# Moving a quarter of the value-row sums from TensorE to VectorE in a PEER decoder kernel

## The chip, the cores and the metric

The kernel runs on one core of one Trainium2 chip. The metric is the device time in microseconds (us), the median of the runs shown.

## What is computed

The reference is a decoder trunk of two layers over 512 tokens of width 1024, in float32. Layer 0 mixes tokens with gated linear attention (GLA), layer 1 with sliding-window attention (SWA); after each mixer stands a PEER channel mixer. In PEER every token picks, in each of 8 heads, 16 of 16384 experts by a product-key top-k. Expert e has a row u[e] and a row v[e] of 1024 values each. A token's 128 picks give

```python
ue = u[e]
ve = v[e]
a = jax.nn.gelu(jnp.einsum('thkd,td->thk', ue, xb).astype(jnp.float32), approximate=False) * g
return jnp.einsum('thk,thkd->td', a.astype(xb.dtype), ve)
```

So each pick is a dot product with u[e], a scalar coefficient, and a scaled sum of v[e]. The rows differ from token to token, so all of them are gathered from HBM: 512 tokens x 128 picks x 2 layers x 8 KB, some 1074 MB.

## The kernel before

Tokens are in 4 blocks of 128, one token a partition. Each block and layer is a stage, 8 stages in all. A stage has two sides that run beside each other: it serves the picks of its own block, and it prepares the next block (mixer, query projection, top-k selection). The last stage has no preparation.

**Serving.** Tables u and v lie side by side, so a gather brings 8 KB a partition, 1 MB a pick. `ring` has 8 slots for them. A stage's 128 picks are 16 rounds of 8 slots, or 64 beats of 2 picks. For a pick in slot i the engines do this:
- POOL (L497) waits for `used[i]`, which says that the slot is free, and issues the gather. It takes slots in order.
- DVE (L840) waits for `got[i]` and multiplies the u row with `h_now`, with the sum in `dots`.
- ACT makes gelu (L1041), `coef`, which is gelu times gate (L1044), and `diag`, the identity scaled by `coef` (L1052). There are 4 `diag` buffers, so ACT first waits until PE has used the one of four picks ago.
- PE (L1310) multiplies `diag` with the v row in two halves of 512 columns into the PSUM tile `acc`, which gathers the sum of all 128 picks. Its last matmul increments `used[i]`.

**Preparing.** Each engine's steps carry a beat in the table `AT`; `beside` writes them into the engine's instruction stream ahead of that beat's picks, and runs rounds without a step in a hardware loop. Engines run in order, so an engine that waits in a step holds back its picks too. Steps tell each other by `said_by`. Among them are, on PE, the strips of weights (L1119, L1130: 8 or 16 matmul groups on a 1 MB strip), the output projection, whose end is the event `y`, the query projection `pq0` to `pq3` and the scores (L1298), which read `keysT`. On DVE they are the attention scores' mask and maximum (L667 to L683) and the selection from `topa0` to `keyb1` (L745 to L823), at beats 48 to 63 in layer 0 and 51 to 63 in layer 1. The one-hot (L805) and its uses lie in the `arena` at 4096. The attention groups g0 to g3 start at beats 17, 21, 25 and 29.

**Loads.** SP issues the weight strips. 8 are resident in a layer; the rest are streamed through two buffers, each when its predecessor is used or when an event such as `y` is said (`FREED`). `keysT`, 0.5 MB, has an SBUF tile of its own and is loaded once a layer.

## Time and profile before

| | |
|---|---|
| median of 3 runs | 3310.17 us (3306.16 to 3312.98) |
| span of the profiled execution | 3290.3 us |
| mean granted TensorE clock | 0.935 of full |
| data moved by DMA | 1173.69 MB, 357 GB/s on average |
| PE / DVE / ACT / POOL busy | 81% / 57% / 38% / 39% of the span |

The profile is of one execution, and its span goes from the first to the last instruction; the device time contains some 20 us around it. The stages lie in it as follows (first dot of each): stage 0 at 185 us, 1 at 584, 2 at 990, 3 at 1389, 4 at 1790, 5 at 2182, 6 at 2577, 7 at 2970. Stages 0 to 2 prepare a layer-0 block, stages 3 to 6 a layer-1 block. The names of engines are those of the profile: PE is TensorE (PEld its weight loads), DVE VectorE, ACT ScalarE, POOL GpSimd, SP SyncE. A matmul of float32 appears as several MATMUL records. A busy share says little by itself, since the stages have several stretches with different limits.

### The profile page before, as it was taken

Reading aid. Unit: us, or ns where it says so; the run is one execution under the profiler, and the core shown is the slowest. Engines: PE = TensorE matmul, PEld = TensorE weight load, DVE = VectorE, ACT = ScalarE, POOL = GpSimd, SP = SyncE. Lnnn points to the kernel's source line nnn. Section 1 sums busy time; section 2 is a strip of 40 time slices with the busy share of each in tenths; the row PEclk is TensorE's granted clock in tenths of the full one; section 3 lists DMA queues with packets and bytes.
Section 4 is the critical chain, followed back from the end, with each engine's and each line's share of the span. In section 5 each row is a group of like instructions: output and inputs, shape, how many; then the busy total and the mean of one; then the engine's idle time right before and its main releaser. Section 6 shows DMA issues by size and latency. Waiting matters only on the chain.

```text
span 3290.3 us, 33210 instructions
## 1 busy us (share of the span) xinstructions
PE 2668.6 (81%) x8416; PEld 1386.3 (42%) x8416; DVE 1876.9 (57%) x4651; ACT 1239.7 (38%) x3668; POOL 1277.0 (39%) x1186
## 2 busy tenths in 40 slices
PE   7568887888878888688896978878897788978777
PEld 6435453453534544343452434434453344533222
DVE  2564549444494455936468554775448654495444
ACT  2033423334333443335333353344433344333333
POOL 0033433334343343333344333434334343436675
PEclk9789998899989999899998999989999999989999
DMA  5388998989989899899898998989989898999999
GB/s 194 110 351 328 399 376 340 369 333 395 384 352 371 336 401 377 346 421 399 308 412 336 367 383 322 396 340 360 362 336 382 339 382 327 368 368 380 422 422 375
DMA packets 163484, 1173.69 MB, mean 357 GB/s; under 512 B 18848, under 2 KB 19104, under 8 KB 21488
## 3 DMA queue, kind: packets, MB, share of 16 engines
q0 software_dynamic: 147456, 1073.81, 81.7%
q1 hardware_dynamic: 15856, 97.88, 7.4%
q8 instruction: 72, 1.18, 0.1%
q14 instruction: 100, 0.82, 0.1%
HBM read 1167.42 MB, written 4.19 MB: 356 GB/s over the span
## 4 chain that ended last, share of the span: by engine, by line
PE 20%; DVE 14%; issue 6%; POOL 6%; DMA 3%; ACT 2%; ACTq 0%; POOLq 0%; DVEq 0%; SPq 0%
PE acc L1310 14%; POOL ring L497 6%; DVE ring L840 5%; PE ps L1130 3%; DMA ring<-in_uv,pick_now 3%; PE ps L1119 1%; DVE arena L813 1%; DVE arena L805 1%; DVE arena L817 1%; PE ps L1254 1%; DVE arena L757 1%; PE ps L1128 1%; DVE arena L749 1%; DVE arena L750 1%; ACT diag L1052 0%
## 5 line engine op out<-in xcount | busy, mean ns | idle before, releaser
L1310 PE MATMUL acc<-ring,diag 128*128 128x512 f32 x4096 | 1995.1, 635 | 544.8 <-ACT diag L1052 542.3
L497 POOL DMA_INDIRECT ring<-in_uv,pick_now x1024 | 1227.7, 1199 | 1840.7 <-PE acc L1310 1592.9
L840 DVE CUSTOM_DVE_ANT_0 ring<-ring,h_now 128x1024 f32<-128x1024 f32 x1024 | 1228.3, 1223 | 871.5 <-DMA ring<-in_uv,pick_now 861.2
L1310 PEld LDWEIGHTS acc<-ring,diag 128*128 128x128 f32 x4096 | 793.4, 202 | 1637.3 <-issue 830.3
L1041 ACT ACTIVATE gelu<-dots 128x1 f32<-128x1 f32 x1024 | 202.4, 198 | 1091.6 <-DVE dots L840 1080.7
L1052 ACT ACTIVATE diag<-ident,coef 128x128 f32<-128x128 f32 x1024 | 411.1, 401 | 258.8 <-PE acc L1310 218.2
L1044 ACT ACTIVATE coef<-gate,gelu 128x1 f32 (+1 forms) x1024 | 301.5, 294 | 120.1 <-issue 7.0
L1130 PE MATMUL ps<-resident,actT 128*128 128x256 f32 x768 | 176.5, 383 | 0.0
L1130 PEld LDWEIGHTS ps<-resident,actT 128*128 128x128 f32 x768 | 143.2, 190 | 34.0 <-issue 16.4
L1130 PE MATMUL ps<-stream,actT 128*128 128x256 f32 x576 | 132.4, 384 | 5.1 <-DMA stream<-in_strips 2.8
L1119 PE MATMUL ps<-actT,stream 128*128 128x128 f32 x1024 | 123.3, 282 | 9.4 <-ACT actT L906 9.4
L1119 PEld LDWEIGHTS ps<-actT,stream 128*128 128x128 f32 x1024 | 121.6, 198 | 18.3 <-issue 15.3
L1130 PEld LDWEIGHTS ps<-stream,actT 128*128 128x128 f32 x576 | 109.8, 192 | 33.7 <-issue 15.8
L489 POOL COPY pick_now<-pick 128x8 uint32 x128 | 44.6, 348 | 149.1 <-DVE pick L823 148.2
L1041 ACT ACT_TABLE_LOAD x67 | 86.0, 1283 | 10.6 <-issue 9.4
L840 DVE DVE_READ_ACCUMULATOR2_ANT dots<- 128x1 f32 x1024 | 84.2, 82 | 0.0
L667 DVE SCALAR_TENSOR_TENSOR arena<-ps,band 128x1024 f32<-128x1024 f32 x16 | 19.6, 1224 | 105.4 <-PE ps L1234 105.4
L996 ACT ACTIVATE arena<-arena,mx 128x256 f32<-128x256 f32 x64 | 31.7, 497 | 92.1 <-DVE mx L683 92.1
L1119 PEld LDWEIGHTS ps<-actT,resident 128*128 128x128 f32 x512 | 62.1, 200 | 8.6 <-issue 6.0
L1102 PE MATMUL ps<-ident,arena 128*128 128x128 f32 x224 | 34.8, 306 | 37.4 <-DVE arena L608 18.3
L1119 PE MATMUL ps<-actT,resident 128*128 128x128 f32 x512 | 62.5, 283 | 2.3 <-ACT actT L910 2.3
L745 DVE MAX8 arena<-ps 128x8 f32<-128x128 f32 x128 | 26.9, 283 | 63.1 <-PE ps L1298 32.3
(180 smaller groups left out, 1302.0 us busy)
## 6 DMA issues: line engine op xcount, KB each, us to landing
stream<-in_strips SPq DMA_DIRECT2D x68, 1024.0 KB
resident<-in_strips SPq DMA_DIRECT2D x16, 1024.0 KB, 17.9
ring<-in_uv,pick_now POOLq DMA_INDIRECT x1024
xc<-in_x SPq DMA_DIRECT2D x4, 512.0 KB
h<-arena SPq DMA_DIRECT2D x4, 512.0 KB
xc<-h SPq DMA_DIRECT2D x4, 512.0 KB
out<-arena SPq DMA_DIRECT2D x4, 512.0 KB
keysT<-in_keys SPq DMA_DIRECT2D x2, 512.0 KB, 14.7
```

What stands on the lines that cost most here:

```text
L489: step(pool.tensor_copy(pick_now[:, half, :], pick[:, bass.ds((base + pair) * (2 * SLOTS) + (half * SLOTS - layer * BLOCKS * PICKS), SLOTS)]))
L497: pool.indirect_dma_start(ring[:, i, :], None, tables[layer], bass.IndirectOffsetOnAxis(ap=pick_now[:, half, i:i + 1], axis=0),).then_inc( ...
L749: step.mark(dve.max_index(topi[:, v, 0:8], top[:, v, 0:8], score(v)))
L750: step.mark(dve.match_replace(c_rest[:, i], top[:, v, 0:8], score(v), LOWEST))
L840: dve.tensor_tensor_reduce(ring[:, i, 0:D], ring[:, i, 0:D], h_now[:], 1.0, 0.0, ALU.mult, ALU.add, dots[:, i:i + 1]).then_inc(dotted, 1)
L1041: act.activation(gelu[:, i:i + 1], dots[:, i:i + 1], ACT.Gelu).then_inc(gelued, 1)
L1044: act.activation(coef[:, i:i + 1], gate[:, bass.ds(col, 1)], ACT.Copy, scale=gelu[:, i:i + 1]).then_inc(weighed, 1)
L1052: act.activation(diag[:, i % 4, :], ident[:], ACT.Copy, scale=coef[:, i:i + 1]).then_inc(diag_ready, 1)
L1102: i = pe.transpose(ps[:, k // 4, (k % 4) * P:(k % 4 + 1) * P], src[:, k, :], ident[:])
L1119: i = pe.matmul(ps[:, bank, (2 * side + c) * P:(2 * side + c + 1) * P], w[:, k, c * P:(c + 1) * P], actT[:, k, :], start=(k == 0), stop=(k ...
L1130: i = pe.matmul(dst, actT[:, k, :], w[:, k, :], start=(k == 0 and bias is None), stop=(k == KT - 1))
L1310: m = pe.matmul(acc[:, b * 512:(b + 1) * 512], diag[:, i % 4, :], ring[:, i, D + b * 512:D + (b + 1) * 512], start=False, stop=True, skip_ ...
```

## The change

In rounds 0 to 13 of each stage the slots 3 and 7 (`VECTOR`) are no longer PE's. DVE multiplies their v row with `coef` and adds it to `side`, a new SBUF tile of 128x1024, with one `scalar_tensor_tensor` each, and increments `used[i]` itself. ACT makes `gelu` and `coef` for them but no `diag`. In a part of several beats the add comes after the next pick's dot; at the end of a part it comes right behind its own. Before round 15 PE folds `side` into `acc` with the identity (4 more matmul records), and DVE clears `side` at the start of each stage. Rounds 14 and 15 stay with PE.

`side` takes the room of the tile `keysT`, which moves into the `arena` at 4096, where the one-hot also lies. So the keys are loaded once a block (8 times, 2 before), on SP's queue right behind the streamed strip number `KEYS_AT` (9 in layer 0, 2 in layer 1: in both the strip of `pq1`, issued at `y`). PE waits for them ahead of `pq0`. DVE waits for `scores1` before the one-hot of either half.

```diff
+KEYS_AT = tuple(f.index("y") + 2 for f in FREED)
+VECTOR = ((3, 7),) * 14 + ((),) * 2
+TENSOR = tuple(tuple(i for i in range(SLOTS) if i not in v) for v in VECTOR)
+FOLD_AT = 15
@@ tiles
+        side = sb("side", [P, D])
-        keysT = sb("keysT", [P, HEADS_P, KEYS])
+        keysT = area(4096, HEADS_P, KEYS)
@@ SP
-                    if n == 2 and first and prep.layer == 0:
-                        sp.dma_start(keysT[:], keys0).then_inc(keys_loaded, 16)
...
+                    if n == KEYS_AT[prep.layer]:
+
+                        sp.dma_start(keysT, (keys0, keys1)[prep.layer]).then_inc(keys_loaded, 16)
@@ DVE, choose
+                said_by(dve, "pe", prep, "scores1")
@@ DVE, take_h
+                dve.wait_ge(side_folded, s + 1)
+                dve.memset(side[:], 0.0).then_inc(side_cleared, 1)
+                dve.wait_ge(side_cleared, s + 1)
@@ DVE, serve
+                    def add(i):
+                        dve.wait_ge(weighed, (s * ROUNDS + r) * SLOTS + (i + 1))
+                        if i == mine[0]:
+                            dve.wait_ge(used[mine[-1]], s * ROUNDS + (r + 1))
+                        else:
+                            dve.wait_ge(used[mine[mine.index(i) - 1]], s * ROUNDS + (r + 2))
+                        dve.scalar_tensor_tensor(side[:], ring[:, i, D:2 * D], coef[:, i:i + 1], side[:], ALU.mult,
+                                                 ALU.add).then_inc(used[i], 1)
+
                     for i in range(beat * BEAT, (beat + n) * BEAT):
...
+                        if i - 1 in mine and i > beat * BEAT:
+                            add(i - 1)
+                    if i in mine:
+                        add(i)
@@ ACT, serve
+                        if i not in TENSOR[r0]:
+                            continue
@@ PE, select
-                pe.wait_ge(keys_loaded, 16 * (prep.layer + 1))
+                pe.wait_ge(keys_loaded, (prep.p + prep.layer * BLOCKS) * 16 + 16)
@@ PE, serve
+                    if beat == 0 and r0 == FOLD_AT:
+                        fold(s)
...
+                        if i not in TENSOR[r0]:
+                            continue
+            def fold(s):
+
+                last = max(r for r in range(ROUNDS) if VECTOR[r])
+                pe.wait_ge(used[VECTOR[last][-1]], s * ROUNDS + (last + 2))
+                for b in range(2):
+                    m = pe.matmul(acc[:, b * 512:(b + 1) * 512], ident[:], side[:, b * 512:(b + 1) * 512],
+                                  start=False, stop=True, skip_group_check=True)
+                m.then_inc(side_folded, 1)
```

## Rows read from the trace of the kernel before

**Rows 1.** The page: busy times by engine, DMA in 40 slices
```profile
PE 2668.6 (81%) x8416; PEld 1386.3 (42%) x8416; DVE 1876.9 (57%) x4651; ACT 1239.7 (38%) x3668; POOL 1277.0 (39%) x1186
...
DMA  5388998989989899899898998989989898999999
```
**Rows 2.** The page: groups; busy us, mean ns | idle before, releaser
```profile
L1310 PE MATMUL acc<-ring,diag 128*128 128x512 f32 x4096 | 1995.1, 635 | 544.8 <-ACT diag L1052 542.3
L497 POOL DMA_INDIRECT ring<-in_uv,pick_now x1024 | 1227.7, 1199 | 1840.7 <-PE acc L1310 1592.9
L840 DVE CUSTOM_DVE_ANT_0 ring<-ring,h_now 128x1024 f32<-128x1024 f32 x1024 | 1228.3, 1223 | 871.5 <-DMA ring<-in_uv,pick_now 861.2
```
**Rows 3.** Busy time in stretches of stage 1; window: length, engines, clock, DMA, GB/s
```profile
584.00:645.00 61.00, 49.43 (x167) 25.69 (x166) 30.63 (x56) 24.62 (x76) 24.69 (x23) 0.92 0.98 395
645.00:728.20 83.20, 74.20 (x266) 44.75 (x266) 36.13 (x64) 33.61 (x97) 29.44 (x29) 0.94 0.80 301
728.20:889.50 161.30, 142.00 (x463) 76.62 (x461) 68.10 (x124) 58.80 (x174) 60.94 (x58) 0.96 0.99 407
889.50:985.80 96.30, 68.31 (x201) 33.30 (x201) 93.90 (x322) 33.77 (x100) 37.41 (x35) 0.86 0.83 332
```
**Rows 4.** The same for stage 5; engines are PE, PEld, DVE, ACT, POOL
```profile
2225.60:2260.30 34.70, 34.70 (x113) 20.55 (x112) 15.43 (x30) 10.81 (x30) 12.05 (x12) 1.00 0.78 286
...
2295.80:2367.10 71.30, 58.65 (x192) 29.79 (x192) 37.35 (x70) 36.13 (x105) 26.30 (x27) 0.93 0.93 366
2367.10:2448.70 81.60, 72.66 (x220) 38.83 (x220) 34.42 (x70) 28.79 (x86) 27.84 (x29) 0.96 0.82 319
2448.70:2486.00 37.30, 34.98 (x139) 18.94 (x140) 17.08 (x31) 14.98 (x48) 20.92 (x17) 1.00 1.01 421
2486.00:2575.00 89.00, 59.04 (x182) 27.71 (x180) 87.15 (x312) 29.39 (x85) 31.03 (x30) 0.94 0.86 338
```
**Rows 5.** The same for 64 picks of stage 7
```profile
3005.20:3164.90 159.70, 126.82 (x256) 43.20 (x256) 78.90 (x128) 57.50 (x192) 112.35 (x72) 1.00 1.01 422
```
**Rows 6.** Chain that ended last, one attention group: start us, us, what
```profile
2311.73 1.24 DVE arena L667
...
2319.56 5.40 PE acc L1310 x8
...
2325.83 6.87 PE acc L1310 x16
...
2335.54 1.24 DVE arena L667
```
**Rows 7.** Timeline, beat 55 of stage 5: start us, us, instruction
```profile
2514.91 1.16 PE L1298 MATMUL ps<-keysT,arena 64*128 64x128 f32 x16
...
2515.42 1.22 DVE L840 CUSTOM_DVE_ANT_0 ring<-ring,h_now 128x1024 f32<-128x1024 f32 x1
...
2517.23 0.29 ACT L1044 ACTIVATE coef<-gate,gelu 128x1 f32 x1
...
2518.08 1.43 DVE L805 TENSOR_TENSOR arena<-arena,iota 128x256 f32<-128x256 f32 x4
```
**Rows 8.** SCALAR_TENSOR_TENSOR: durations min/median/max by line; a group of the page
```profile
L555 DVE SCALAR_TENSOR_TENSOR arena<-arena x4: 691/692/693, 38.5 to 1076.9; 128x512 f32<-128x512 f32 x4
...
L667 DVE SCALAR_TENSOR_TENSOR arena<-ps,band 128x1024 f32<-128x1024 f32 x16 | 19.6, 1224 | 105.4 <-PE ps L1234 105.4
```
**Rows 9.** The keys: landing (page, part 6), SP's strip and PE's `pq0` (timeline)
```profile
keysT<-in_keys SPq DMA_DIRECT2D x2, 512.0 KB, 14.7
...
2440.03 20.11 SPq L403 DMA_DIRECT2D stream<-in_strips  x3
...
2448.94 3.83 PE L1119 MATMUL ps<-actT,stream 128*128 128x128 f32 x32 [1.20 <-ACT actT L906]
```
**Rows 10.** Busy time in stretches: late in the selection of stage 1
```profile
933.10:959.90 26.80, 13.94 (x19) 5.78 (x20) 26.36 (x101) 7.18 (x24) 4.27 (x6) 0.62 0.62 247
```

More of the change, by code:

```diff
@@ L42, with turns @@
 GAIN_AT = (6, 2)
+KEYS_AT = tuple(f.index("y") + 2 for f in FREED)
 BEAT = 2
 BEATS = PICKS // BEAT
+VECTOR = ((3, 7),) * 14 + ((),) * 2
+TENSOR = tuple(tuple(i for i in range(SLOTS) if i not in v) for v in VECTOR)
+FOLD_AT = 15
+def turns(upto, r0, of):
+    return sum(len(p) for p in of[:r0]) + (upto - r0) * len(of[r0])
+TENSOR_TURNS = sum(len(p) for p in TENSOR)
+VECTOR_TURNS = sum(len(p) for p in VECTOR)
 AT = {
@@ L205, in build @@
         seeded = sem("seeded")
+        side_cleared = sem("side_cleared")
+        side_folded = sem("side_folded")
         acc_taken = sem("acc_taken")
@@ L328, in serve @@
                     r, beat = divmod(done, per)
-                    if beat == 0 and until - done >= 2 * per:
-                        n = (until - done) // per
+                    n = 0
+                    if beat == 0:
+                        while done + (n + 1) * per <= until and VECTOR[r + n] == VECTOR[r] and (not n or FOLD_AT not in (r, r + n)):
+                            n += 1
+                    if n >= 2:
                         alone(eng, anchor)
                         with eng.Fori(r, r + n) as rr:
-                            half(rr, 0, per)
+                            half(rr, r, 0, per)
                         done += n * per
@@ L336, in serve @@
                         n = min(per - beat, until - done)
-                        half(r, beat, n)
+                        half(r, r, beat, n)
                         done += n
@@ L373, in load_block @@
                     sp.dma_start(bias_in, b_in).then_inc(small_loaded, 16)
-                if first and prep.layer == 1:
-                    said_by(sp, "pe", Prep("gla", BLOCKS - 1), "scores1")
-                    sp.dma_start(keysT[:], keys1).then_inc(keys_loaded, 16)
             def load_kept(prep):
@@ L876, in _ @@
             dve.sem_inc(dotted, 1)
+            dve.sem_inc(side_folded, 1)
             for beat in preps(Prep("gla", 0)):
@@ L1036, in serve, with part @@
             def serve(s):
-                def part(r, beat, n):
+                def part(r, r0, beat, n):
                     for i in range(beat * BEAT, (beat + n) * BEAT):
```

11 lines of the change are left out of this document (6 added, 5 removed).

## Prediction

> **What bounds the kernel now.** I read the page's busy times first. TensorE (PE) is busy 81% of the span and VectorE (DVE) 57%, and the DMA engines are at nine tenths in most slices [rows 1]. No one of them is at its limit all the time, so I read which wait is last in which stretch. The group table says who waits for whom: GpSimd (POOL), which issues the gathers, stood idle 1593 us for PE's matmuls on `acc`, because a ring slot comes free when PE has used it [rows 2]. Then I cut one stage of each layer into stretches. Three regimes appear.
>
> - The last stage has no preparation beside it. Its 64 picks from 3005.2 to 3164.9 take 2.50 us each at 422 GB/s and a DMA share of 1.01, with PE busy 127 of 160 us [rows 5]. This is the DMA's limit: 2.5 us for a pick's 1 MB.
> - In a stage with preparation, PE has the weight strips too. Where DMA share is below 1 here, the ring is full of rows that PE has not used. Stage 1 (layer 0 prepared beside it): share 0.80 in 645 to 728.2, nearly full before and after. Stage 5 (layer 1): 0.78, 0.93 and 0.82 in three stretches [rows 3, 4].
> - At the end of each such stage DVE runs the top-k selection beside its dots. It is busy 93.9 of 96.3 us in stage 1 and 87.2 of 89.0 in stage 5, with DMA at 0.83 and 0.86 [rows 3, 4]. DVE is the bound there.
>
> The change thus takes work from the engine that bounds the second regime and gives it to the engine that bounds the third.
>
> **What it takes from PE.** One pick on PE is 16 matmul records for 4 picks in 6.87 us, so 1.72 us [rows 6]. Per stage 28 of 128 picks leave PE: 8 x 28 x 1.72 = 385 us of PE work. Most of it is not on the path: stage 7 is DMA-bound (0), and in the selection DVE decides (0). In the rest I count stretch by stretch, never more than the DMA's idle share, since a transfer-bound stretch cannot get shorter.
>
> Layer 1 beside stage 5 (and 3, 4, 6 alike):
> - 2225.6 to 2260.3: PE never idle, DMA idle 0.22 x 34.7 = 7.6 us. One round's two picks: 2 x 1.72 = 3.4 us.
> - The attention groups, 23.8 us each. The chain of waits gives the loop: scores end at 2311.7, DVE masks and takes the maximum, ScalarE (ACT) does the exponentials, reloads its table and makes the next diagonal, PE starts again at 2319.56, does two picks in 5.40 us, transposes, four picks in 6.87 us, and the next scores release DVE at 2335.54 [rows 6]. Groups start at beats 17, 21, 25 and 29, so of the two VECTOR picks of a loop slot 3 lies in the 8 us in which PE waits for DVE and ACT anyway, and only slot 7 is among the six on the path: 1.72 us a loop. Three loops lie in 2295.8 to 2367.1, where DMA is idle 0.07 x 71.3 = 5.0 us: 5.0. The fourth: 1.7.
> - 2367.1 to 2448.7: DMA idle 0.18 x 81.6 = 14.7 us, PE idle 8.9. Six picks leave; I count five on the path, 8.6 us.
> - 2448.7 to 2486: DMA share 1.01, nothing.
> Sum 18.7 us, times 4 = 75 us.
>
> Layer 0 beside stage 1 (and 0, 2 alike): 645 to 728.2 has DMA idle 0.20 x 83.2 = 16.6 us; six of the removed picks fall where PE is late for the gate projection or catches up after it, 10.3 us. 728.2 to 889.5 is at 0.99: 1.5 us. Sum 11.8, times 3 = 35 us.
>
> Gain: 110 us. The bounds are 0 and the whole DMA idle time of these stretches, 27.3 x 4 + 18.2 x 3 = 164 us.
>
> **What it gives to DVE.** The new multiply-add over 128x1024 f32 from SBUF doesn't occur in this trace. The same operation over 512 elements takes 0.69 us from SBUF, and over 1024 elements with a PSUM input 1.22 us [rows 8]; the dots take 1.22 us [rows 2]. The two points of the first operation lie on a line through about 1.04 ns an element, so I take 1.22 us (bounds 1.1 and 1.4). Before it DVE must wait for ACT's `coef` of the same pick. Where selection steps cut a round into beats, the add stands right behind its own dot. In beat 55 of stage 5 the second dot ends at 2516.64 and its `coef` at 2517.52 [rows 7]: 0.9 us of wait. In quieter beats I take 0.7 us, because two short ACT instructions follow a dot. Selection begins at beat 51 in layer 1 and 48 in layer 0. So three adds (slots 7, 3, 7) lie in it in layer 1: 3 x 1.22 + 0.7 + 0.7 + 0.9 = 6.0 us. Layer 0 has four, the first with a dot between and no wait: 7.2 us. Total 4 x 6.0 + 3 x 7.2 = 46 us (bounds 30 without any wait, 70 with an additional microsecond each). Outside selection DVE is busy less than half of the time, and its adds are covered as long as ACT isn't late.
>
> **The smaller parts.**
> - Keys per block: six more loads of 0.5 MB. At 422 GB/s that is 1.24 us each, 7.5 us, on the path because the load falls in a stretch that is at 1.01 [rows 4]. The same load also adds a wait: PE now needs it before `pq0`, behind strip `pq1` on SP's queue. In stage 5 that strip is issued at 2440.03 and PE starts `pq0` at 2448.94 [rows 9]. If the strip lands after some 8 us and the keys after 2.5 us more at half the rate, PE stalls some 2 us, with its picks queued behind, and POOL behind them. PE has one pick less in that stretch, so I count 0 (bound: the 14.7 us that an earlier keys load took to land, less 8.9, in 4 blocks: 23 us). In layer 0 the selection chain is longer and there is no stall. SP waits for nothing new.
> - DVE's new wait for `scores1` before the one-hot: scores end at 2516.07 and the one-hot starts at 2518.08, and DVE has two adds more ahead of it: 0.
> - ACT saves 224 diagonals; it is not the bound: 0. The fold is one pick's work, 1.7 us, in round 15 where PE is idle a third of the time [rows 3]: 0. Clearing `side` lies at a stage's start, where DVE is busy 31 of 61 us [rows 3]: 0, at most 8 x 1.2 us.
> - Coupling: DVE could run eight picks ahead of PE. Now an add needs ACT's `coef`, and ACT is held within four diagonals of PE. After each point at which ACT waited, the next dot comes later by the add. In the attention loop that is 0.3 us after `pT`. As an estimate, some five such points of 0.3 us in each of seven stages are 10 us (bounds 0 and the third rival).
>
> **The sum.** -110 + 46 + 7.5 + 10 = -46 us. Against the profiled execution (span 3290.3) that is 3244; the median of the runs is 3310.2, 20 us above that span, which stay: 3264 us.
>
> **The rivals.**
> - Deeper gain: the DMA closes nearly all its idle time ahead of the selection, since all slot-7 picks and part of the slot-3 ones were late. -164 + 46 + 7.5 = -110 us: 3200. For it: POOL's 1593 us of waiting for PE. Against it: latency loops as [rows 6] contain waits that no lighter PE removes.
> - Slower, by DVE held behind ACT: in every round beside preparation, an add that waits for `coef` keeps back the next dot, and from that `coef` PE's next diagonal needs 1.22 (add) + 1.14 (dot) + 1.0 (ACT's three steps) = 3.4 us, while PE may have one pick, 1.7 us, in hand. A bubble of 1.2 us, a value between 0 and that 1.7 us, in each of 12 rounds of 7 stages is 101 us: -56 + 101 = +45 us, 3355. It decides from 56 / 84 = 0.67 us a round. Against it: with three diagonals ready, PE has 5.2 us in hand.
> - The clock: PE's granted clock was 0.62 where it was busy 13.9 of 26.8 us [rows 10], and after each 4 us of waiting in the attention loop two picks cost 5.40 instead of 3.43 us [rows 6]. The change makes PE idler. Two more such restarts of 2.0 us a stage in 7 stages are 28 us, and stage 7 at the lower of the two levels (1.2 against 2.4 GHz) would need 6 x 3.43 = 20.6 us a round against 20.0, 8 us more: -46 + 36 = -10 us, 3300. The Trainium skill, "TensorE: Matmul & The Clock Gate", section "HAM oscillation — how this bites in real kernels", states that a PE that waits between bursts starts each burst at the lower clock; by that rule this rival holds. Stage 7 at 1.00 with PE a fifth idle [rows 5] speaks against it there.
> - No change: the picks that leave PE lie in waits, and only half of the 110 us comes through: +9 us or, with no coupling, -1 us: 3310.
>
> **Chances.** Forecast 0.52, deeper gain 0.15, slower 0.17, clock 0.08, no change 0.08. The forecast's own range is 3225 to 3300. With a tenth left out on each side the range is 3200 to 3340. A measurement here tells 0.2%, 7 us. Faster: 0.50 + 0.15 + 0.05 = 0.70; same 0.10; slower 0.20.
>
> **What would show it.** DVE busy up by 224 x 1.22 = 273 us and PE down by some 370. Stretches before the selection 12 to 19 us shorter, selections 6 to 7 us longer, stage 7 unchanged. A wait of the new line on `coef` of over 150 us in total, with PE idle for `diag`, would prove the slower rival right; more time at the lower clock in stage 7 the clock's. A stall of over 5 us at `pq0` on the keys would break my 0 there.

## The result and the profile after

The changed kernel takes 3323.7 us (median of 4 runs, 3323.2 to 3324.9) against 3309.2 us for the kernel before on the same chip (4 runs, 3306.2 to 3313.0). The ratio is 1.0047 [1.0033, 1.0061]: slower by 0.5%. The forecast was 3264 us, faster. The time lies in the range, the sign is wrong.

The profiled spans are 3321.9 and 3290.3 us, which is 31.6 us apart where the medians are 14.5 apart. The span of after lies 1.7 us below the time of that same run (3323.6), and in every run below that has both, the time lies 1.7 to 2.2 us above the span. So there are not 20 us around a span, as my sum had it: the profiled execution of before, whose own time is not on record, must have been some 17 us faster than the median of its runs. A difference between the profile of before and that of after is therefore too large by some 17 us in all, and the sizes below come from medians where it matters. The kernel before took medians of 3304.5 to 3309.2 us on the chips of the runs below, so each kernel is also given as a ratio to before on its own chip. The reading of where time lies comes from the profiles.

The page of after, lines that answer to [rows 1, 2], with the new line L866 last:

```profile
PE 2430.3 (73%) x7552; PEld 1281.1 (39%) x7552; DVE 2154.9 (65%) x4883; ACT 1160.1 (35%) x3444; POOL 1264.8 (38%) x1186
...
PEclk9789888998878988888888888888898888988888
DMA  4389988999879998799898998989988898989999
...
L1353 PE MATMUL acc<-ring,diag 128*128 128x512 f32 x3200 | 1730.3, 690 | 779.8 <-ACT diag L1091 778.2
L514 POOL DMA_INDIRECT ring<-in_uv,pick_now x1024 | 1184.6, 1157 | 1885.9 <-PE acc L1353 1608.6
L872 DVE CUSTOM_DVE_ANT_0 ring<-ring,h_now 128x1024 f32<-128x1024 f32 x1024 | 1225.1, 1222 | 550.0 <-DMA ring<-in_uv,pick_now 535.0
L866 DVE SCALAR_TENSOR_TENSOR side<-ring,coef,side 128x1024 f32<-128x1024 f32 x224 | 287.6, 1284 | 285.7 <-ACT coef L1081 285.7
```

The same clock line of the kernel before:

```profile
PEclk9789998899989999899998999989999999989999
```

DVE is up by 278 us (forecast 273). PE is down by 238 us where 370 were forecast, because each record that is left got longer: mean 635 to 690 ns, at a lower clock (the granted clock over the whole span is 0.87 where it was 0.94). PE's idle time for `diag` rose from 542 to 778 us. And DVE waits 285.7 us for `coef` ahead of its additions. POOL still waits 1.6 ms for PE.

The stretches of after: stage 1 up to its selection and the selection; stage 5 up to DVE's first addition on `xc`, from there to the selection, and the selection; then most of stage 7 (length, busy us of PE, PEld, DVE, ACT, POOL, clock, DMA share, GB/s):

```profile
585.30:882.10 296.80, 230.78 (x796) 130.07 (x796) 163.77 (x267) 109.30 (x322) 115.61 (x108) 0.91 0.96 388
882.10:991.00 108.90, 71.31 (x196) 33.91 (x196) 100.50 (x329) 33.06 (x99) 39.08 (x37) 0.81 0.79 309
2203.30:2455.00 251.70, 196.21 (x579) 102.33 (x578) 151.84 (x260) 102.51 (x305) 100.84 (x95) 0.88 0.92 357
2455.00:2505.30 50.30, 37.42 (x140) 21.95 (x139) 27.65 (x46) 17.87 (x51) 21.87 (x20) 0.83 1.00 410
2505.30:2604.00 98.70, 63.64 (x182) 29.39 (x180) 92.68 (x318) 29.09 (x85) 32.06 (x31) 0.86 0.82 313
3036.00:3197.00 161.00, 109.80 (x195) 40.78 (x193) 99.15 (x147) 51.58 (x178) 87.86 (x74) 0.87 1.01 422
```

The three parts of stage 5 in the kernel before, cut at the same instructions ([rows 4] has other cuts):

```profile
2182.40:2440.00 257.60, 220.92 (x658) 114.39 (x657) 126.44 (x240) 110.22 (x329) 96.69 (x95) 0.94 0.89 351
2440.00:2486.00 46.00, 42.72 (x164) 22.56 (x163) 22.96 (x42) 18.54 (x52) 24.75 (x20) 1.00 1.01 422
2486.00:2577.20 91.20, 61.21 (x187) 28.77 (x186) 87.91 (x314) 30.29 (x88) 31.96 (x30) 0.94 0.86 335
```

The first part lost 25 us of PE's work and is 5.9 us shorter, not 18.7. The second is 4.3 us longer. The selection is 7.5 us longer. The sixth row of after is the clock's test: 422 GB/s, share 1.01 as in [rows 5], at clock 0.87 instead of 1.00, and stage 7 takes 319.8 us in whole where before takes 320.2. (A stage begins with its first dot.)

The same cuts through every stage, worked out from the traces ("to y" ends at DVE's first addition on `xc`, the selection begins with its first maximum search and ends with the stage; sums over stages 0 to 6, us). The other kernels are explained below:

| kernel | to y | y to selection | selections | stage 7 | span |
|---|---|---|---|---|---|
| before | 1849.6 | 275.3 | 660.0 | 320.2 | 3290.3 |
| after | 1820.3 | 282.2 | 714.4 | 319.8 | 3321.9 |
| keys only | 1857.0 | 303.2 | 663.1 | 320.8 | 3328.2 |
| relief only | 1784.5 | 282.7 | 673.9 | 319.4 | 3245.9 |
| additions only | 1877.8 | 294.6 | 723.9 | 318.9 | 3401.7 |
| rounds 0 to 11 | 1823.1 | 278.3 | 669.9 | 319.4 | 3275.6 |
| no wait for own `coef` | 1794.1 | 282.9 | 702.5 | 319.9 | 3285.6 |

So two readings suggest themselves: the selections are 54 us longer (forecast 46), and ahead of them only 22 us come back, or up to 39 if all the 17 us of the fast profile of before lie there. Which term took the rest of the 110 us was the question for the runs.

### The profile page after: what moved, and what is told of

Read it like the earlier page. It is cut to its first block, busy times and chain, and to the rows that moved or that the text cites. A ratio compares the mean times of both kernels' runs of the same rounds, so it can differ in the third digit from the quotient of the medians.

```text
span 3321.9 us, 31399 instructions
## 1 busy us (share of the span) xinstructions
PE 2430.3 (73%) x7552; PEld 1281.1 (39%) x7552; DVE 2154.9 (65%) x4883; ACT 1160.1 (35%) x3444; POOL 1264.8 (38%) x1186
## 4 chain that ended last, share of the span: by engine, by line
PE 18%; DVE 14%; DMA 9%; issue 5%; ACT 4%; POOL 2%; ACTq 0%; DVEq 0%; POOLq 0%; SPq 0%
PE acc L1353 11%; DMA ring<-in_uv,pick_now 7%; DVE ring L872 5%; PE ps L1169 3%; POOL ring L514 2%; DMA arena<-in_keys 1%; PE ps L1158 1%; ACT coef L1081 1%; DVE arena L831 1%; ACT diag L1091 1%; DVE arena L823 1%; DVE side L866 1%; PE ps L1293 1%; ACT gelu L1078 1%; DVE arena L835 1%
## 5 line engine op out<-in xcount | busy, mean ns | idle before, releaser
L1353 PE MATMUL acc<-ring,diag 128*128 128x512 f32 x3200 | 1730.3, 690 | 779.8 <-ACT diag L1091 778.2
L514 POOL DMA_INDIRECT ring<-in_uv,pick_now x1024 | 1184.6, 1157 | 1885.9 <-PE acc L1353 1608.6
L872 DVE CUSTOM_DVE_ANT_0 ring<-ring,h_now 128x1024 f32<-128x1024 f32 x1024 | 1225.1, 1222 | 550.0 <-DMA ring<-in_uv,pick_now 535.0
L1353 PEld LDWEIGHTS acc<-ring,diag 128*128 128x128 f32 x3200 | 671.7, 220 | 1721.5 <-ACT diag L1091 1015.2
L866 DVE SCALAR_TENSOR_TENSOR side<-ring,coef,side 128x1024 f32<-128x1024 f32 x224 | 287.6, 1284 | 285.7 <-ACT coef L1081 285.7
L1091 ACT ACTIVATE diag<-ident,coef 128x128 f32<-128x128 f32 x800 | 321.2, 401 | 161.4 <-PE acc L1353 127.6
L1158 PE MATMUL ps<-actT,stream 128*128 128x128 f32 x1024 | 128.5, 289 | 22.6 <-DMA arena<-in_keys 13.5
L506 POOL COPY pick_now<-pick 128x8 uint32 x128 | 75.4, 589 | 147.9 <-DVE pick L841 147.1
L1141 PE MATMUL ps<-ident,arena 128*128 128x128 f32 x224 | 41.6, 347 | 58.0 <-DVE arena L625 29.8
L1141 PEld LDWEIGHTS ps<-ident,arena 128*128 128x128 f32 x224 | 35.1, 181 | 76.6 <-DVE arena L625 32.8
```

Source lines behind the costliest of these rows:

```text
L506: step(pool.tensor_copy(pick_now[:, half, :], pick[:, bass.ds((base + pair) * (2 * SLOTS) + (half * SLOTS - layer * BLOCKS * PICKS), SLOTS)]))
L514: pool.indirect_dma_start(ring[:, i, :], None, tables[layer], bass.IndirectOffsetOnAxis(ap=pick_now[:, half, i:i + 1], axis=0),).then_inc( ...
L866: dve.scalar_tensor_tensor(side[:], ring[:, i, D:2 * D], coef[:, i:i + 1], side[:], ALU.mult, ALU.add).then_inc(used[i], 1)
L872: dve.tensor_tensor_reduce(ring[:, i, 0:D], ring[:, i, 0:D], h_now[:], 1.0, 0.0, ALU.mult, ALU.add, dots[:, i:i + 1]).then_inc(dotted, 1)
L1091: act.activation(diag[:, i % 4, :], ident[:], ACT.Copy, scale=coef[:, i:i + 1]).then_inc(diag_ready, 1)
L1141: i = pe.transpose(ps[:, k // 4, (k % 4) * P:(k % 4 + 1) * P], src[:, k, :], ident[:])
```

## The experiments

My theory after the result: each term has its own size and the terms add up, the relief being smaller and the additions dearer than forecast, by DVE's waits for `coef`. The rivals: the keys' wait, the clock, or a relief that is worth nothing at all.

### One part at a time

**Keys only.** The keys' table is loaded per block, PE does all picks, DVE adds none.

```diff
-VECTOR = ((3, 7),) * 14 + ((),) * 2
+VECTOR = ((),) * 16
```

(the fold and the clearing of `side` are out as well)

> The keys part alone: the keys lie in the arena and are loaded once a block, and all picks stay with PE; no adds, no side, no fold. Theory A (the picks' move is what costs): the six more loads are 7.5 us, so about 3317 us, against 3309 of before. Rival K (the keys' wait ahead of pq0 costs): in the four layer-1 blocks PE stands 4 us or more with the gathers behind it, which gives 3325 us or more, that is, all of the loss of the change.

3327.8 us (3325.5 to 3335.0), 1.0067 [1.0042, 1.0092]: +20.6 us where I had 7.5. Around `pq0` of stage 5 in this kernel: SP's strip and keys, PE's projection, and the page's landing line (KB, median us):

```profile
2465.32 0.35 SPq L417 DMA_DIRECT2D stream<-in_strips  x1
2465.72 0.43 SPq L421 DMA_DIRECT2D arena<-in_keys  x1
...
2478.38 3.80 PE L1155 MATMUL ps<-actT,stream 128*128 128x128 f32 x18 [5.34 <-DMA arena<-in_keys]
...
arena<-in_keys SPq DMA_DIRECT2D x8, 512.0 KB, 12.4
```

The table is issued 0.4 us after the strip and lands a median 12.4 us later, beside gathers that hold the DMA at its limit. PE stands 5.34 us in front of `pq0` with its picks queued behind. In the four layer-1 blocks `pq0` starts 4.0 to 5.3 us later, counted from y, than before; in stage 5 that is 4.15, since before already waited 1.20 us for ACT there [rows 9]. In the changed kernel, with one pick less there, the wait of stage 5 is still 3.88 us, that of stage 6 is 6.2, and it is 13.5 us in all (17.2 in keys only). PE in the changed kernel, and its group on the page:

```profile
2467.16 5.80 PE L1158 MATMUL ps<-actT,stream 128*128 128x128 f32 x32 [3.88 <-DMA arena<-in_keys]
...
L1158 PE MATMUL ps<-actT,stream 128*128 128x128 f32 x1024 | 128.5, 289 | 22.6 <-DMA arena<-in_keys 13.5
```

**Relief only.** As after, with no addition on DVE: the v rows of slots 3 and 7 are left out of the sum, and ACT releases the slots in DVE's stead. The fold and the clearing of `side` stay.

```diff
-                        if i - 1 in mine and i > beat * BEAT:
-                            add(i - 1)
-                    if i in mine:
-                        add(i)
...
                         if i not in TENSOR[r0]:
+                            act.sem_inc(used[i], 1)
                             continue
```

> The changed kernel without DVE's adds: PE and ACT leave slots 3 and 7 of rounds 0 to 13 out, as in the change, but nobody adds their v rows (that part of the result is left out), and ACT frees their slots. It measures what the relief of PE is worth by itself, with the keys part in it. My forecast's term: 110 us of gain less 7.5 for the keys, so about 3207 us. Theory C (the clock: a PE with less to do waits longer, drops to the lower clock more often and does its remaining picks slower): half or more of the gain is missing, 3260 us or more, with time at the lower clock before each selection near the 75 us of the changed kernel. Theory B (DVE is held by the wait for coef) has nothing to act on here and expects 3207.

3253.1 us, 0.9843 [0.9821, 0.9864]. Against keys only that is -74.6 us: the relief's price by itself (with the fold and the clearing in it), where 110 were forecast.

**Additions only.** PE does all picks again, DVE adds those of slots 3 and 7 too. The additions have semaphores of their own, and POOL waits for them as well.

```diff
-TENSOR = tuple(tuple(i for i in range(SLOTS) if i not in v) for v in VECTOR)
+TENSOR = (tuple(range(SLOTS)),) * 16
...
+                                if i in added:
+                                    pool.wait_ge(added[i], n + 1)
```

> DVE does all adds of the change into side, but PE keeps all eight picks of each round and nothing is folded, so the result is unchanged; a ring slot waits for both. It measures what the adds cost by themselves, with the keys part in it. Forecast's terms: 46 us in the selections and 7.5 for the keys, so about 3363 us. Theory B (the wait for coef also makes dots late outside the selection): 3390 us or more, and idle time of over 200 us ahead of the adds. Theory C: about 3363 to 3370, with the granted clock at before's 0.93.

3400.4 us, 1.0279 [1.0257, 1.0301]: +72.6 us over keys only, where 46 + 10 = 56 were forecast. DVE waited 338 us for `coef` here:

```profile
DVE side L870 <- ACT coef L1088: 338.3, 168, 13.7
```

The three add up: 20.6 - 74.6 + 72.6 = +18.6 us; the whole change measured +14.5. The clearing of `side` is in two of the three prices. No large interaction is left, and the relief is real. That rules out the rival that it is worth nothing.

### The selection

**Rounds 0 to 11.** DVE's additions end before the selection begins, and the picks of rounds 12 and 13 go back to PE.

```diff
-VECTOR = ((3, 7),) * 14 + ((),) * 2
+VECTOR = ((3, 7),) * 12 + ((),) * 4
```

> The change with VECTOR rounds 0 to 11 in place of 0 to 13, so that the selections, where DVE is busy all the time, have no adds (in layer 1 at all, in layer 0 none after the scores). Measured lengthening of a selection in the changed kernel is 7 to 8.6 us in 7 stages, 54 us. If that is a loss of its own, 3324 - 54 = 3270 us, faster than before by 1.2%. If the moved picks' PE time comes back onto the path in rounds 12 and 13 instead, 3300 us or more.

3278.1 us, 0.9914 [0.9893, 0.9934]: 45.7 us less than after. The table shows where: selections 714.4 to 669.9, the rest within 4 us. Moving the picks of rounds 12 and 13 too turns a gain of 0.9% into a loss of 0.5%. This term was forecast at 46.

### The wait for coef

Waits of after (us in total, times, longest us):

```profile
POOL ring L514 <- PE acc L1353: 1608.6, 530, 27.0
...
PE acc L1353 <- ACT diag L1091: 778.2, 259, 53.1
...
DVE side L866 <- ACT coef L1081: 285.7, 161, 12.3
...
POOL ring L514 <- DVE side L866: 68.0, 32, 10.1
```

And DVE at the start of stage 5, where five dots run, and the addition of the fourth (slot 3) stands behind the fifth:

```profile
2209.16 1.22 DVE L872 CUSTOM_DVE_ANT_0 ring<-ring,h_now 128x1024 f32<-128x1024 f32 x1
...
2213.66 1.28 DVE L866 SCALAR_TENSOR_TENSOR side<-ring,coef,side 128x1024 f32<-128x1024 f32 x1 [3.27 <-ACT coef L1081]
...
2222.74 1.29 DVE L866 SCALAR_TENSOR_TENSOR side<-ring,coef,side 128x1024 f32<-128x1024 f32 x1 [1.89 <-ACT coef L1081]
```

DVE had run up to its fifth dot, and then stood 3.27 us for ACT, which had started on the first pick of the stage only at 2209.98 and took 0.98 us for each. In the kernel before ACT was as late there; DVE ran on to its sixth dot and then stood 9.57 us for a step of ACT, so at this place the new wait need not cost anything. What it costs elsewhere is that the next dot stands behind DVE's addition, and the next diagonal behind the dot.

What ACT did in the 285.7 us, summed from its own row in the trace: 182 us it made `gelu`, `coef` and `diag` of the picks it was behind with, 39 us it stood for PE's matmuls of the preparation, 31 us it was in its own steps of the preparation, table loads among them, and only 2.7 us it stood for a diagonal buffer that PE had not used. The rest are short gaps between its instructions. So in these waits it was ACT's own work and steps that DVE waited for, hardly the limit of four diagonals.

**No wait for its own coef.** The addition takes 1.0 as its scalar and waits for the `coef` two picks earlier. The sum is then not the weighted one.

```diff
-                        dve.wait_ge(weighed, (s * ROUNDS + r) * SLOTS + (i + 1))
+                        dve.wait_ge(weighed, (s * ROUNDS + r) * SLOTS + (i - 1))
...
-                        dve.scalar_tensor_tensor(side[:], ring[:, i, D:2 * D], coef[:, i:i + 1], side[:], ALU.mult,
+                        dve.scalar_tensor_tensor(side[:], ring[:, i, D:2 * D], 1.0, side[:], ALU.mult,
```

(in rounds 14 and 15 the dots of slots 3 and 7 wait for ACT's count too)

> The changed kernel with DVE's add scaled by 1.0 and waiting for the coef of the pick two earlier, so that it hardly waits for ACT (the sum in side is then not the weighted one; the work and its order stay). Theory B (the slower rival: the wait for coef holds DVE, 286 us in all): the adds cost 70 us in the changed kernel, 41 in the selections and 35 ahead of them; 224 adds of 1.28 us explain 28 adds x 1.2 us = 34 us in the selections, so the waits would be the rest, and 20 to 35 us go: 3290 to 3304 us. If the adds' own time is what costs, 3316 us or more.

3285.8 us, 0.9938 [0.9919, 0.9957]: 38 us less than after, with as many additions and in the same places. By the table 26 us of it lie ahead of y and 12 in the selections. Its additions, and its waits:

```profile
L866 DVE SCALAR_TENSOR_TENSOR side<-ring,side 128x1024 f32<-128x1024 f32 x224 | 273.7, 1222 | 38.7 <-ACT coef L1083 38.7
```

```profile
PE acc L1355 <- ACT diag L1093: 746.0, 263, 52.2
...
DVE ring L874 <- DMA ring<-in_uv,pick_now: 674.3, 439, 4.7
...
DVE side L866 <- ACT coef L1083: 38.7, 33, 3.3
```

The wait for `coef` has shrunk from 286 to 39 us, and DVE again waits for the gathers (674 us, after 535): it runs ahead. But the edit also made each addition shorter, 1222 ns for 1284, because its scalar is no longer read from a tile: 14 us of DVE's time in all. So the wait is worth 24 to 38 us, as an estimate from the two; no run separates them. The part of it ahead of the selection is the coupling for which I took 10 us.

**Slots 2 and 6.** In the rolled rounds the addition of a slot stands behind the next slot's dot, but that of slot 7 stands right behind its own dot. Slots 2 and 6 both have a dot in between.

```diff
-VECTOR = ((3, 7),) * 14 + ((),) * 2
+VECTOR = ((2, 6),) * 14 + ((),) * 2
```

> The changed kernel with slots 2 and 6 in place of 3 and 7, so that another dot always stands between a pick's dot and its add, and the diagonals that ACT makes ahead of a coef are fewer by one. Theory B (DVE's wait for coef, 286 us in total, is on the path): the wait falls by 100 us or more, and the time by 20 us or more, to 3304 or less, the most of it in the selections. If the wait only takes the place of waits for DMA and PE, the time stays at 3318 to 3326.

3321.1 us, 1.0034 [1.0022, 1.0046], against 1.0047 [1.0033, 1.0061]: no difference that these intervals can tell.

```profile
POOL ring L514 <- DVE side L866: 273.8, 91, 17.0
DVE side L866 <- ACT coef L1081: 198.2, 75, 12.9
```

DVE's wait fell from 286 to 198 us, and POOL's wait for DVE's release of the slot rose from 68 to 274 us. The wait was moved, not removed. By the same cuts the selections of this kernel are 17 us shorter than after's (697.8) and its time to y is 15 us longer (1835.0).

**Slot 3 alone and slot 7 alone**, each in rounds 0 to 11.

```diff
-VECTOR = ((3, 7),) * 14 + ((),) * 2
+VECTOR = ((3,),) * 12 + ((),) * 4
...
                         elif i < 4:
                             act.wait_ge(used[i + 4], s * ROUNDS + r + 1)
+                        elif i == 7:
+                            act.wait_ge(used[7], s * ROUNDS + r + 1)
```

(slot 7 alone is the mirror image: `((7,),) * 12` and a further wait on `used[3]` for slot 3)

> Only slot 3 goes to DVE, in rounds 0 to 11; ACT's wait for slot 7's diagonal buffer is set to slot 7 itself. With both slots these rounds gave 3278 us, 49 us less than the keys alone (3328). If each slot is worth half, 3303 us. If slot 3 lies in PE's waits of the attention groups, as I forecast, slot 3 gives less than slot 7: 3305 to 3315 us.

> Only slot 7 goes to DVE, in rounds 0 to 11; ACT's wait for slot 3's buffer is for slot 3 itself. By my forecast slot 7 lies on the path of the attention groups and gives the larger part: 3290 to 3298 us. But the traces of the change show PE waiting for ACT right behind slot 6 there, because ACT copies the transposed weights and reloads tables before it serves the next pick; then slot 7's removal only lengthens that wait, and slot 7 is worth no more than slot 3: 3303 us or more.

Slot 3 alone: 3290.4 us, 0.9949 [0.9934, 0.9965], which is 37 us below keys only. Slot 7 alone: 3315.5 us, 1.0029 [1.0015, 1.0043], 12 us below it. Together 49, as rounds 0 to 11 has them (3278.1). Waits for `coef`, of slot 3 alone and then of slot 7 alone:

```profile
DVE side L866 <- ACT coef L1081: 106.8, 48, 6.9
```

```profile
DVE side L866 <- ACT coef L1081: 221.7, 95, 11.0
```

The same 96 additions wait twice as long where no dot stands between. These two runs carry relief and additions together, so they do not say how the 25 us between them divide; that stays open. It is the reverse of the order that I expected. By the traces, as means of stages 4 to 6 against keys only, slot 7 alone gave more in the three attention loops (3.3 against 0.6 us), but in the stretch ahead of them it was 0.7 us longer where slot 3 was 4.6 shorter, and from the last group to y 0.6 longer where slot 3 was 1.8 shorter.

### Where the relief went

The same two kernels show the attention loop of [rows 6] with one pick taken out at a time. First PE in the kernel before, in the loop and in front of the last burst:

```profile
2319.56 5.40 PE L1310 MATMUL acc<-ring,diag 128*128 128x512 f32 x8 [4.24 <-ACT diag L1052]
...
2378.53 3.70 PE L1310 MATMUL acc<-ring,diag 128*128 128x512 f32 x8 [1.65 <-ACT diag L1052]
```

PE in stage 5, slot 3 alone:

```profile
2308.03 1.98 PE L1355 MATMUL acc<-ring,diag 128*128 128x512 f32 x4
2315.97 5.42 PE L1355 MATMUL acc<-ring,diag 128*128 128x512 f32 x8 [5.96 <-ACT diag L1093]
...
2339.80 5.45 PE L1355 MATMUL acc<-ring,diag 128*128 128x512 f32 x8 [5.96 <-ACT diag L1093]
```

PE in stage 5, slot 7 alone, the same place in four successive loops, and the last loop's end:

```profile
2308.76 5.15 PE L1355 MATMUL acc<-ring,diag 128*128 128x512 f32 x8 [4.24 <-ACT diag L1093]
...
2331.21 5.40 PE L1355 MATMUL acc<-ring,diag 128*128 128x512 f32 x8 [4.24 <-ACT diag L1093]
...
2339.53 3.70 PE L1355 MATMUL acc<-ring,diag 128*128 128x512 f32 x8 [0.34 <-ACT diag L1093]
...
2353.90 6.46 PE L1355 MATMUL acc<-ring,diag 128*128 128x512 f32 x8 [4.24 <-ACT diag L1093]
...
2377.74 6.49 PE L1355 MATMUL acc<-ring,diag 128*128 128x512 f32 x8 [4.24 <-ACT diag L1093]
...
2390.19 5.40 PE L1355 MATMUL acc<-ring,diag 128*128 128x512 f32 x8 [3.37 <-ACT diag L1093]
```

Slot 3's pick lay in the wait for the softmax: PE's wait went from 4.24 to 5.96 us, by just the pick's 1.72, and the loop stayed at 23.8 us. Slot 7's was on the path in two loops, 2331.21 - 2308.76 = 22.45 us and then 22.69; the third, 23.84 us, gained nothing. So far the forecast is right in the main. But with both out, relief only, PE in stage 5:

```profile
2254.64 6.29 PE L1350 MATMUL acc<-ring,diag 128*128 128x512 f32 x8 [5.96 <-ACT diag L1088]
...
2263.86 3.70 PE L1350 MATMUL acc<-ring,diag 128*128 128x512 f32 x8 [0.34 <-ACT diag L1088]
...
2278.23 6.44 PE L1350 MATMUL acc<-ring,diag 128*128 128x512 f32 x8 [5.96 <-ACT diag L1088]
...
2301.98 6.51 PE L1350 MATMUL acc<-ring,diag 128*128 128x512 f32 x8 [5.97 <-ACT diag L1088]
...
2338.34 5.40 PE L1350 MATMUL acc<-ring,diag 128*128 128x512 f32 x8 [3.37 <-ACT diag L1088]
```

The loop is 23.6 and 23.75 us, and 23.81 in before. The 1.72 us came out, 0.9 to 1.1 went back into the two picks behind the wait (5.40 to 6.29, 6.44 and 6.51 us), and 0.6 at the new wait for a diagonal (0.34 us of it shown as the wait). The longer wait alone does not lengthen those two picks: slot 3 alone has the same 5.96 us of wait and 5.42 us behind it, and slot 7 alone has before's 4.24 us and 6.46 and 6.49 in its third and fourth loop. What differs is the granted clock over the two picks, 0.68 in before and with slot 3 alone, 0.56 to 0.58 in the others. In these runs it goes with slot 7's pick missing from the work between two waits, though keys only shows it in stage 4 as well (6.50 and 5.99 us); what sets it was not tried. And in front of the last burst PE ran out of work: where before had two picks in front of ACT's table loads and waited 1.65 us, there is now one pick and a wait of 3.37, and the two picks after it take 5.40 instead of 3.70 us.

Against keys only, as means of stages 4 to 6, three loops gave 1.3 us (forecast 5.0; stage 4 of keys only had two slow loops, and in stages 5 and 6 it is 0.4), the stretch from the last group to y 2.4 (forecast 10.3), and the stretch from the stage's start to the first group 9.5 (forecast 3.4): 13.1 us of the 18.7. In stages 0 to 2 the time to y fell by 8.9 us (forecast 11.8), and in stage 3 by 6.4 (forecast 18.7). From y to the selection, where I had counted nothing in layer 1 and 1.5 us at most in layer 0, the relief gave 20.5 us in all, 16 of them in the three blocks of layer 0. The selections of relief only were 10.8 us longer than those of keys only, so a part was given back; what in them takes it was not tried.

### The keys' wait

**Keys at the scores**: PE waits for the table where it first reads it, ahead of the scores, not ahead of `pq0`.

```diff
-                pe.wait_ge(keys_loaded, (prep.p + prep.layer * BLOCKS) * 16 + 16)
                 for b in range(2):
...
                     said_by(pe, "act", prep, f"pq{b}")
+                    if b == 0:
+                        pe.wait_ge(keys_loaded, (prep.p + prep.layer * BLOCKS) * 16 + 16)
```

> The changed kernel with PE's wait for the keys moved from ahead of pq0 to ahead of the first scores, which is the first step that reads them. The load stays as it is, so its traffic is paid. With the keys alone, PE started pq0 4.2 to 5.3 us later after the second norm than before in each of the four layer-1 blocks, 18 us. If that stall lies on the path, as the 20.6 us of the keys part say, 3324 - 17 = 3307 us. If it is the traffic or the SP queue that costs, 3320 us or more.

3320.1 us, 1.0037 [1.0022, 1.0053]: 3.6 us less than after, which the intervals can't tell from nothing. The stretch from y to the selection in stage 5 with it:

```profile
2450.50:2500.00 49.50, 37.10 (x143) 19.64 (x142) 27.67 (x46) 18.09 (x51) 20.57 (x21) 0.93 1.01 422
```

It is still at 422 GB/s with a share of 1.01, and 3.5 us longer than before. The table's 0.5 MB is 1.24 us of that at this rate; that the transfer decides the rest too is a reading, not shown.

**Keys only, waited for at the scores**: the first kernel with the same edit.

> The keys alone, all picks on PE, with PE's wait for the keys ahead of the first scores in place of ahead of pq0. If the stall at pq0 costs when PE has its full load: 3307 + 20.6 - 4 x 3 = about 3315 us. If the 20.6 us are traffic and what the load displaces in a stretch in which the DMA is the limit, the time stays at 3324 or more, as it nearly did in the changed kernel (3 to 4 us less).

3316.9 us, 1.0032 [1.0018, 1.0047], against 1.0067 [1.0042, 1.0092]. The medians lie 10.8 us apart, the intervals just overlap, and the profiles agree in place and size: y to selection 303.2 to 292.4 us. So some 8 to 11 us of the keys' 20.6 are the stall at `pq0`; 12.4 are left. Six tables at full rate are 7.5 us. What the other 5 are was not tried, but the profiles say where to look: the stretch from y to the selection fell from 203.1 to 192.6 us in the four layer-1 blocks (before: 186.0) and stayed at 100 us in the three of layer 0 (before: 89.3), where my forecast had no cost but the traffic.

### The clock

Bursts behind a wait run in part at the lower level, 1.2 of 2.4 GHz: the granted clock was 0.68 over the 5.40 us of [rows 6] and 1.00 in the wait before them and in the work behind. To price this I had PE work through its known waits: four matmuls of 512 columns with a zero tile as weights, into the same accumulator, in each of the 16 attention groups.

```diff
+                    yield at[f"g{g}"] + 1
+                    for _ in range(4):
+                        pe.matmul(acc[:, 0:512], zero,
+                                  ident[:].rearrange("p (o n) -> p o n", o=1).to_broadcast([P, 4, P]),
+                                  start=False, stop=True, skip_group_check=True)
```

> The changed kernel with four more matmuls of a zero 128x128 tile with the identity repeated to 512 columns, added to acc (they add nothing), in each attention group of layer 1, at the place where PE has done its picks and waits 6 us for DVE and ACT. Theory C (the clock): PE's next two picks take 3.4 to 4 us instead of 6.1, the time at the lower clock before a layer-1 selection falls from 75 to under 50 us, and a group from 23.5 to some 21.5 us; 16 groups, 20 to 35 us in total, 3290 to 3304 us. If the lower clock isn't what holds PE, the extra matmuls cost nothing or up to 1 us a group: 3324 to 3340 us.

> The kernel before with the same extra zero matmuls in the 16 attention groups. There PE waits 4.2 us in a group and the two picks behind the wait take 5.40 us. If the lower clock costs the kernel before as well, each takes 3.4 to 3.7 and a group comes down from 23.8 to 22 us, where the DMA's 93% leave 1.7 us a group: 10 to 25 us less, about 3290 us. If the lower clock matters only with the lighter PE of the change, 3305 to 3315 us.

> PE's relief alone, with the keys part (slots 3 and 7 of rounds 0 to 13 are left out of the sum), and the extra zero matmuls. The relief was worth 75 us where I forecast 110. If the lower clock took the rest, 20 us or more come back: 3233 us or less. If the DMA is the limit once PE is relieved, nothing comes back: 3248 to 3256 us.

After with zeros: 3301.6 us, 0.998 [0.997, 0.999], so -22. Before with zeros: 3277.3 us, 0.9927 [0.9909, 0.9945], so -27 by the medians of its chip. Relief only with zeros: 3225.5 us, 0.9764 [0.9746, 0.9782], so -28. By the ratios the three are -22, -24 and -26 us. One attention group of before with zeros, PE: the zero matmuls, and the two picks behind the wait:

```profile
2320.85 3.60 PE L1243 MATMUL acc<-ident,past 128*128 128x512 f32 x8
...
2325.26 3.70 PE L1318 MATMUL acc<-ring,diag 128*128 128x512 f32 x8 [0.82 <-ACT diag L1055]
```

PE adds 3.60 us of work that computes nothing, and the two picks behind it take 3.70 us, not 5.40; the loop is 22.1 us, not 23.8. The Trainium skill, "TensorE: Matmul & The Clock Gate", section "HAM oscillation — how this bites in real kernels", describes matmul bursts between waits that start at the lower clock each time. The trace agrees: 5.40 and 6.44 us against 3.70 for the same two picks.

The loss in these waits is real, and what the zeros give back is about equal in both kernels (22 against 27 us), so it does not explain why after is slower. Nor does it explain the relief: with zeros in both it is worth 3225.5 against 3277.3, -52 us with the keys' share in it, and without zeros 3253.1 against 3307.1, -54 us.

This does not clear the clock as a whole. In before the zeros brought all 16 bursts to 3.70 us; in after 7 of 16 still took 5.40, in relief only 4 of 16. And the 16 waits are a small part: by the granted clock (twice its missing share, times the stretch), the time at the lower level ahead of y, stages 0 to 6, is 188 us in before and 401 in after, and with zeros 136 and 344. What the 200 us more in after cost was not tried, so part of the relief's missing 35 us may be theirs.

### What is left when the causes are put right

**Rounds 0 to 11 with the keys at the scores**, and then **with the zero matmuls** too.

> Rounds 0 to 11 only and the wait for the keys at the scores: both repairs at once. If the costs add, 3278 - 17 = 3261 us, faster than before by 1.4%. If the selection is then the next limit for what the keys' wait gives, 3270 us or more.

> Rounds 0 to 11, the keys' wait at the scores, and the extra zero matmuls. If the parts add, 3276 - 22 = 3254 us, 1.6% faster than before. If the DMA takes part of it, 3262.

3276.1 us, 0.9898 [0.988, 0.9916], and 3257.6 us, 0.9861 [0.9845, 0.9878]. The later wait for the keys gave 2 us on top of rounds 0 to 11 where I had 17, which can't be told from nothing. The last kernel is 1.4% faster than the kernel before. The zeros alone bring before to 0.9927, so the moved picks, with the keys' loads paid, are worth the remaining 0.7%.

## Why the prediction was wrong

The medians give +14.5 us where the sum was -46. The miss of 61 us by its terms, each from a run that has that term alone:

| term | forecast | measured | by |
|---|---|---|---|
| relief of PE | -110 | -75 | relief only less keys only |
| additions on DVE and coupling | +46 + 10 | +73 | additions only less keys only |
| keys per block | +7.5 | +21 | keys only less before |
| sum | -46 | +19 | the whole change: +14.5 |

No one term turns the sign by itself: with the relief as forecast, or without the moved picks of rounds 12 and 13 (measured, -46), or without DVE's wait for `coef` (measured, -38 with the shorter additions), the kernel would be faster than before. In place of the gain of 46 us stand a relief 35 us too large, keys 13 too small, and additions with their coupling 17 too small.

**The three regimes: right.** PE decides ahead of the selection, DVE in it, the DMA in stage 7. Stage 7 lost a quarter of PE's picks and stayed at 320 us.

**Relief: right in mechanism, a third too large.** The step that failed is "only slot 7 is among the six on the path: 1.72 us a loop", priced at the clock of [rows 6]. Slot 3 in the shadow and slot 7 on the path in two loops of three are both shown. But each was judged with the other still in place and at an unchanged clock. With both gone the two picks behind the wait take 0.9 to 1.1 us more, at a granted clock of 0.56 to 0.58 for 0.68, a new wait takes 0.6, and of the 1.72 us there remain 0.2 at most. The second step is "six picks leave; I count five on the path, 8.6 us" in the stretch behind the loops: 2.4 us came for 10.3 (with the fourth loop's 1.7), as one of those picks only stood in front of ACT's table loads. In the other direction, the stretch ahead of the groups gave 9.5 us for my 3.4: I had counted one round's two picks, between 2225.6 and 2260.3, and left out the rest of a stretch of over 100 us. In all the profiles give 72 us to y and 20 from there to the selection, and take 11 back in the selections, 82 where the medians give 75. How much the lower clock took outside the attention groups stays open.

**Selection: right in size, with some luck.** 46 us forecast; 46 us came back when these additions were taken out and their picks given back. The addition takes 1.28 us where I had 1.22, and a row of the kernel before that I had not used says so: the same operation over 1024 elements with its scalar in a tile.

```profile
L724 DVE SCALAR_TENSOR_TENSOR arena<-xc,stat,ps 128x1024 f32<-128x1024 f32 x8 | 10.2, 1280 | 0.3
```

Beside a full PE the additions lengthen the selections by 61 us (additions only less keys only, profiles), beside a relieved one by 41 (after less relief only); the relief by itself had already put 11 into them, which my sum had at nothing.

**Coupling: the effect named, the size missed.** I took 10 us from "some five such points of 0.3 us". Taking most of the wait away gives 38 us, up to 14 of them by the shorter addition. 12 of the 38 lie in the selections, whose 46 us held some 16 of waiting; ahead of them it is 26 us for my 10. The 0.3 us was the delay of a dot by one addition. What DVE loses is its lead: it stands up to 12.3 us, and its wait for the gathers, 861 us in before, fell to 535. The reason that I gave, "ACT is held within four diagonals of PE", is not what the trace shows: 2.7 of the 285.7 us fall in such a wait, while ACT is behind by its own work of some 1 us a pick and by steps of the preparation.

The slower rival had this effect and set its own test, a wait of over 150 us on `coef` with PE idle for `diag`. The trace has 286 us and 778 us for 542, so by that test it was right, and its +101 us were too many: the 286 us of waiting cost 24 to 38. That PE had diagonals in hand for the rest, as I had argued against it, fits this but was not counted. Its 56 / 84 = 0.67 us a round as the point from which it decides assumed the full 110 us of relief and 7.5 for the keys.

**Keys: the step "PE has one pick less in that stretch, so I count 0" failed.** I had the strip land after some 8 us and the table 2.5 later; the table landed 12.4 us after its issue. The stall at `pq0` was 5.3 us in stage 5 of keys only, and 3.9 with the pick less. The 5 us that were to break the 0 were reached in one block of the changed kernel, 6.2 us in stage 6. That the stall cost time is shown with all picks on PE (8 to 11 us); in the changed kernel taking it away gave 3.6 us, which is not clear of the noise. "In layer 0 the selection chain is longer and there is no stall" holds as to the stall, but the stretch there is 11 us longer in the three blocks of keys only, cause open. My bound of 23 us for it, beside the 7.5 for the traffic, held.

**Clock rival: part refuted, part open.** More time at the lower level is there, 868 us of after's span against 431 by the granted clock, but at the attention groups the zeros give after no more back than before. Its 8 us in stage 7 did not come: PE is busy 110 of 161 us there at 0.87. Elsewhere its price was not measured.

**"20 us around the span".** The profiled execution of before was a fast one; 1.7 to 2.2 us lie around a span. This shifted no sign, as the forecast was the median less 46.

## What to carry to other kernels

Price work that is handed to another engine by the lead that the taker loses, not by its busy time: ask how far it ran ahead and whose result it must now wait for. Price relief for all removed pieces at once and at the clock that the idler engine will get: in stages 5 and 6 slot 7's picks alone gave 2.7 us in three loops, slot 3's nothing, and both together 0.4. And when a load moves next to a strip in a stretch at 422 GB/s, its waiter should be the instruction that reads it; that gave 8 to 11 us where PE had its full load, and nothing clear of the noise where it had not. A second edit inside an experiment, here a scalar that is no longer read from a tile, can be worth a part of what the experiment measures, so look at the row of the edited instruction too.

## What the runs showed of the hardware

- Zero matmuls in PE's known waits keep the clock for the work behind them: 3.60 us of them turn two picks of 5.40 us into 3.70, at all 16 places in the kernel before, which gains 27 us. In the changed kernel 9 of the 16 came to 3.70.
- The length of a wait does not settle what the work behind it costs: two picks took 5.42 us behind 5.96 us of waiting (slot 3 alone) and 6.46 behind 4.24 (slot 7 alone).
- A lower clock costs nothing where the DMA decides: stage 7 takes 319.8 us at clock 0.87 and 320.2 us at 1.00.
- A multiply-add over 128x1024 f32 takes 1284 ns all from SBUF, and 1280 with a PSUM input (L724), where its scalar is read from a tile; with a constant as its scalar it takes 1222 ns from SBUF (no wait for own `coef`) and 1224 with a PSUM input [rows 8].
- A 0.5 MB table issued 0.4 us behind a 1 MB strip, beside saturating gathers, lands a median 12.4 us after its issue.
